# Expert layers: 32 x 32 turns on VectorE, stripes of 1024 hidden columns, longer runs in the weight loads

## Chip, cores and metric

One core of a Trainium2 chip runs the kernel. The metric is the device time of one execution in microseconds; the time before is the median of three runs.

## The reference

A decoder trunk of two layers on one sequence of 256 tokens with 1024 channels, all in float32. Each layer has a mixer part (a gated convolution, a state-space model and a sparse attention side by side, merged by gates) and then a feed-forward part. The first layer's is dense. The second layer's, which the change touches, sends each token to two of eight experts:

```python
def swiglu(h, w1, w3, w2):
    return (jax.nn.silu(h @ w1) * (h @ w3)) @ w2

def moe_ffn(h, router_w, w1, w3, w2):
    logits = (h @ router_w).astype(jnp.float32)
    vals, idx = lax.top_k(logits, TOP_K_EXPERTS)          # 2 of 8
    probs = jax.nn.softmax(vals, axis=-1)
    gate = jnp.sum(jax.nn.one_hot(idx, N_EXPERTS, dtype=jnp.float32) * probs[..., None], axis=-2)
    out = jnp.zeros_like(h)
    for e in range(N_EXPERTS):
        out = out + gate[..., e:e + 1] * swiglu(h, w1[e], w3[e], w2[e])
    return out
```

w1 and w3 of an expert are 1024 x 3584, w2 is 3584 x 1024: 44 MB an expert, 352 MB in all.

## The kernel before

The engines run programs of their own and meet through semaphores. SyncE loads all weights in 1 MB chunks into `raw`, a ring of six slots (`load_at`, L595): a slot is loaded again when `used` says that TensorE is done with it. A chunk of w1 or w3 holds 4 of the 8 blocks of 128 input channels by 512 hidden columns, so a partition gets four runs of 2 KB; a chunk of w2 holds 2 blocks of 128 hidden channels by 1024 outputs, two runs of 4 KB.

An expert takes at most 96 tokens (`SLOTS`). Its 3584 hidden columns are cut into 7 stripes of 512. TensorE's order for a stripe is: products with w1 (2 chunks, into bank 0 of PSUM), then the turn of the hidden values of the stripe before (`turn_hidden`, L1364: three 128 x 128 transposes through PSUM bank 4), products with w3 (2 chunks, bank 1), then the down products with w2 for the stripe before (2 chunks, banks 2 and 3, summed over all stripes). ScalarE applies silu to bank 0 (`silu`, L1886); VectorE multiplies by bank 1 (`times_up`, L2444) and copies the turned values from bank 4 to `hidT` (L2591). The first w1 and w3 stripe of the next expert come ahead of the last down products of an expert.

All products are made of `four_tiles`: the 96 tokens are three groups of 32 columns of the array. Each takes 384 of the 512 weight columns (L1333); the remaining 128 columns of all three groups go, one after the other, through the fourth 32 columns (L1336). The four parts of the array work side by side. Values thus lie in PSUM as three rows of tiles of 384 columns and a fourth with three times 128. A float32 matmul shows as two in the profile.

The tokens of the next expert: VectorE makes `pick`, TensorE finds their numbers in the second stripe (`find_tokens`), VectorE casts them (L2587), GpSimd gathers the rows from memory into `xg_tok` (L2909), and TensorE turns them behind w3 of the last stripe of an expert (`turn_gathered`, L1425: eight transposes into banks 6 and 7, copied to `xgT` by ScalarE and VectorE). An expert's output is copied to `y_sb` by ScalarE and stored to `y_rows` by GpSimd (L2835); for the last expert the stored rows of the others are gathered into `y_back` (L2916) and added by VectorE (`add_rows`), and its own output goes back through a scatter product. Rounds after the first (`rnd > 0`) run only if an expert has over 96 tokens. `y_taken`, `hid_done`, `sil_done` and `hidT_copied` guard the buffers.

## Time and profile before

| | us |
|---|---|
| median of three runs | 1647.84 (1646.87 to 1651.17) |
| the profiled execution, its time | 1651.2 |
| its span | 1649.4 |
| TensorE busy | 1614.8 |
| VectorE busy | 582.3 |
| ScalarE busy | 397.8 |
| GpSimd busy | 404.5 |
| first expert matmul | 714.41 |

Busy time of TensorE counts a matmul from start to modelled end, so that a stretch of 100% still has room. The DMA share counts the time of packets over 16 engines; packets in flight overlap, so it can stand above 1. In every slice from 700 us on the expert stage runs. How long a weight transfer takes to land, against how long the slot's turn lasts, tells how late the weights are.

### The profile page before, as it was taken

The page shows a single profiled execution, that of the slowest core. Times are in us where ns is not written, and L with a number is a line of the kernel's source. Part 1 is how long each engine was busy: PE and PEld are TensorE (multiplying, and loading weights), DVE is VectorE, ACT ScalarE, POOL GpSimd, SP SyncE. Part 2 cuts the span into 40 slices and gives each one's busy share as a digit, 9 for nine tenths or more (in the row PEclk, how much of TensorE's full clock was granted, in tenths as well). Part 3 has the DMA queues.
Part 4 walks back from the last instruction along what each step waited for, and adds up shares of the span by engine and source line. Part 5 has one row for each costly group of instructions (what it writes and reads, how often), then busy time and mean ns, then how long its engine had stood idle before and what let it go on. Part 6 is the DMA issues. An engine that isn't in the chain of part 4 may idle for free.

```text
span 1649.4 us, 46626 instructions
## 1 busy us (share of the span) xinstructions
PE 1614.8 (98%) x20940; PEld 1498.3 (91%) x20940; DVE 582.3 (35%) x784; ACT 397.8 (24%) x527; POOL 404.5 (25%) x541
## 2 busy tenths in 40 slices
PE   8999999999999999999999999999999999999998
PEld 5887888999978788899999999999999999999997
DVE  4799866466568977510000000000000000000002
ACT  4245455544454554510000000000000000000000
POOL 8856900999434523120000000000000000000100
PEclk9899999999999999999999999999999999999999
DMA  8453456556544455389999999999999999999996
GB/s 298 130 177 128 145 176 229 186 195 206 179 154 129 147 173 178 120 293 374 392 387 387 390 391 387 387 387 393 389 387 395 385 389 392 389 386 391 395 394 255
DMA packets 212094, 481.10 MB, mean 292 GB/s; under 512 B 7936, under 2 KB 32640, under 8 KB 211696
## 3 DMA queue, kind: packets, MB, share of 16 engines
q1 hardware_dynamic: 207456, 463.34, 77.4%
q0 software_dynamic: 4064, 14.95, 2.7%
q8 instruction: 122, 2.00, 0.5%
q10 hardware_dynamic: 432, 0.65, 0.1%
q14 instruction: 20, 0.16, 0.0%
HBM read 472.49 MB, written 6.42 MB: 290 GB/s over the span
## 4 chain that ended last, share of the span: by engine, by line
PE 67%; DVE 2%; DMA 1%; ACT 0%; issue 0%; DVEq 0%
PE ps L1336 33%; PE ps L1333 20%; PE ps L676 2%; PE ps L677 2%; PE ps L678 2%; PE ps L1364 2%; DMA raw<-moe_w 1%; PE ps L722 1%; PE ps L723 1%; PE ps L724 1%; DVE w_lo L306 1%; PE ps L912 0%; PE ps L1425 0%; PE ps L1300 0%; PE ps L1406 0%; DVE keybias L2169 0%
## 5 line engine op out<-in xcount | busy, mean ns | idle before, releaser
L1336 PE MATMUL ps<-raw,xgT 128*32 128x128 f32 x5424 | 611.6, 273 | 0.0
L1333 PE MATMUL ps<-raw,xgT 128*32 128x384 f32 x5424 | 604.2, 487 | 1.6 <-DMA raw<-moe_w 1.6
L1336 PEld LDWEIGHTS ps<-raw,xgT 128*32 128x32 f32 x5424 | 587.5, 110 | 0.0
L1336 PE MATMUL ps<-raw,hidT 128*32 128x128 f32 x2640 | 297.5, 273 | 0.0
L1333 PE MATMUL ps<-raw,hidT 128*32 128x384 f32 x2640 | 293.9, 486 | 0.0
L1336 PEld LDWEIGHTS ps<-raw,hidT 128*32 128x32 f32 x2640 | 287.5, 110 | 0.0
L306 DVE TENSOR_TENSOR w_lo<-raw,w_hi 128x2048 fp32r<-128x2048 f32 (+1 forms) x97 | 238.3, 2465 | 114.2 <-ACT w_hi L300 113.6
L2591 DVE COPY hidT<-ps 128x384 f32<-128x384 f32 x55 | 30.7, 558 | 564.1 <-PE ps L1364 564.1
L300 ACT ACTIVATE w_hi<-raw 128x2048 fp32r<-128x2048 f32 (+1 forms) x97 | 185.2, 1910 | 174.9 <-PE ps L678 83.4
L1333 PEld LDWEIGHTS ps<-raw,xgT 128*32 128x32 f32 x5424 | 215.9, 109 | 10.1 <-issue 9.8
L1886 ACT ACTIVATE sil<-ps 128x384 f32<-128x384 f32 (+1 forms) x67 | 33.9, 506 | 736.9 <-PE ps L1336 736.9
L2835 POOL DMA_DIRECT2D y_rows<-y_sb x7 | 3.8, 545 | 618.3 <-ACT y_sb L1976 618.3
L2444 DVE TENSOR_TENSOR hid<-sil,ps 128x384 f32<-128x384 f32 (+1 forms) x67 | 38.5, 574 | 279.6 <-PE ps L1336 277.3
L676 PE MATMUL ps<-w_hi,hT_hi 128*128 128x512 f32 (+1 forms) x264 | 105.7, 401 | 3.9 <-DVE uv L2155 3.2
L1333 PEld LDWEIGHTS ps<-raw,hidT 128*32 128x32 f32 x2640 | 106.8, 109 | 1.0 <-issue 0.2
L677 PE MATMUL ps<-w_lo,hT_hi 128*128 128x512 f32 (+1 forms) x264 | 103.8, 393 | 0.0
L678 PE MATMUL ps<-w_hi,hT_lo 128*128 128x512 f32 (+1 forms) x264 | 103.7, 393 | 0.0
L1224 PE MATMUL ps<-hT_hi,w_hi 128*128 128x256 f32 x336 | 95.2, 283 | 0.0
L1226 PE MATMUL ps<-hT_hi,w_lo 128*128 128x256 f32 x336 | 95.1, 283 | 0.0
L1228 PE MATMUL ps<-hT_lo,w_hi 128*128 128x256 f32 x336 | 95.1, 283 | 0.0
L722 PE MATMUL ps<-hT_hi,w_hi 128*128 128x256 f32 x224 | 64.9, 290 | 2.4 <-DVE w_lo L306 2.4
L676 PEld LDWEIGHTS ps<-w_hi,hT_hi 128*128 128x128 f32 x264 | 50.2, 190 | 16.1 <-DVE uv L2155 3.6
(417 smaller groups left out, 2253.1 us busy)
## 6 DMA issues: line engine op xcount, KB each, us to landing
raw<-moe_w SPq DMA_DIRECT2D x336, 1024.0 KB, 9.8
raw<-w_in SPq DMA_DIRECT2D x44, 1024.0 KB, 5.6
raw<-ffn_w SPq DMA_DIRECT2D x33, 1024.0 KB, 5.3
raw<-w_o SPq DMA_DIRECT2D x8, 1024.0 KB, 4.9
raw<-w_out_a SPq DMA_DIRECT2D x4, 1024.0 KB, 4.8
raw<-w_out_c SPq DMA_DIRECT2D x4, 1024.0 KB, 5.0
raw<-w_out_b SPq DMA_DIRECT2D x4, 1024.0 KB, 4.9
raw<-w_in SPq DMA_DIRECT2D x4, 904.0 KB, 4.8
```

The source lines that it names most:

```text
L300: act.activation(w_hi[:, n % SPLIT, 0:width], raw[:, n % RAW, 0:width], ACT.Copy)\
L306: dve.tensor_tensor(w_lo[:, n % SPLIT, 0:width], raw[:, n % RAW, 0:width], w_hi[:, n % SPLIT, 0:width].bitcast(F32), ALU.subtract)\
L676: pe.matmul(dst, x_hi, hi, start=first, stop=False, skip_group_check=True)
L677: pe.matmul(dst, x_hi, lo, start=False, stop=False, skip_group_check=True)
L678: return pe.matmul(dst, x_lo, hi, start=False, stop=last, skip_group_check=True)
L722: pe.matmul(dst, wh, x_hi[:, k0 + k, :], start=start, stop=False, skip_group_check=True)
L1224: pe.matmul(dst, hi[:, k, cols], hT_hi[:, k, :], start=k == 0 and c == 0, stop=False, skip_group_check=True)
L1226: pe.matmul(dst, lo[:, k, cols], hT_hi[:, k, :], start=False, stop=False, skip_group_check=True)
L1228: mm = pe.matmul(dst, hi[:, k, cols], hT_lo[:, k, :], start=False, stop=k == KD - 1, skip_group_check=True)
L1333: pe.matmul(ps[tile_rows(g), bank, 0:WIDE], x_of(g), w[:, 0:WIDE], start=first, stop=last, skip_group_check=True, tile_position=(0, TILE * g))
L1336: mm = pe.matmul(ps[SLOTS:P, bank, g * P:(g + 1) * P], x_of(g), w[:, WIDE:HALF], start=first and g == 0, stop=last, skip_group_check=True, ...
L2444: dve.tensor_tensor(hid[:, 0:width], sil[:, 0:width], ps[:, 1, 0:width], ALU.mult)\
```

## The change

- `HALVES = (2, 2, 2, 1)`: an expert has three stripes of 1024 hidden columns (pairs of halves of 512) and one of 512. TensorE's order for a pair is w1 (4 chunks, banks 0 and 1), w3 (4 chunks, banks 2 and 3), then the down products of the stripe before (4 chunks, or 2 for the half one; banks 4 and 5). SiLU and product take a pair in one instruction.
- The turns of hidden values and gathered rows leave TensorE. VectorE turns blocks of 32 by 32 from `hid_pair` to `hidT` (24 instructions of 32 x 128 for a pair) and from `xg_tok` to `xgT` (12 of 32 x 256).
- Chunks of w1 and w3 in pairs are 2 blocks of 128 input channels by 1024 columns (two runs of 4 KB a partition); the half stripe keeps 4 by 512. Chunks of w2 put four neighbouring hidden channels on one partition and take two of them (one run of 8 KB); the source of the turn is read with a stride of four to match.
- Down products are cut 388 + 3 x 124 in place of 384 + 3 x 128. Rank, token and pick banks move (2 to 4, 5 to 7), and the loops over stripes are written out.

```diff
-MOE_STRIPES = FF_EXPERT // HALF
+PAIR = 2 * HALF
+HALVES = (2, 2, 2, 1)
+MOE_STRIPES = len(HALVES)
+Y_WIDE = WIDE + 4
...
-            w2e = moe_w2[0].rearrange("e (k p) n -> p (e k) n", p=P)
+            w2e = moe_w2[0].rearrange("e (k p j) n -> p (e k) j n", p=P, j=4)
                 def up(m, turns, w, e, t):
-                    col = value(sp, t * HALF)
-                    for half in range(2):
-                        row = value(sp, KD * e + 4 * half)
-                        load_at(m + half, turns, w[:, bass.ds(row, 4), bass.ds(col, HALF)], used)
+                    ks = 4 // HALVES[t]
+                    for c in range(KD // ks):
+                        row = value(sp, KD * e + ks * c)
+                        load_at(m + c, turns, w[:, bass.ds(row, ks), t * PAIR:t * PAIR + HALVES[t] * HALF], used)
                 def down(m, turns, e, t):
-                    for half in range(2):
-                        row = value(sp, K2 * e + 4 * t + 2 * half)
-                        load_at(m + half, turns, w2e[:, bass.ds(row, 2), :], used)
+                    for c in range(2 * HALVES[t]):
+                        row = value(sp, K2 * e + 2 * t + c // 2)
+                        j = 2 * (c % 2)
+                        load_at(m + c, turns, w2e[:, bass.ds(row, 1), j:j + 2, :].rearrange("p o j n -> p (o j) n"),
+                                used)
...
-                def step(i, turns, middle=None, after=None):
-                    up(n0 + 4, 0, i + 1, turns)
-                    turn_hidden(i)
-                    if middle is not None:
-                        middle()
-                    up(n0 + 6, 1, i + 1, turns)
-                    if after is not None:
-                        after()
+                def step(n, i, turns, halves):
+                    up(n, 0, i + 1, turns, halves)
+                    up(n + 2 * halves, 1, i + 1, turns, halves)
                 def expert(e, last):
...
+                    step(n, i, turns, 2)
...
+                    down(n + 8, i + 1, turns, 2, first=True)
+                    n += 12
+                    step(n, i + 1, turns, 2)
+                    if not pick_turned:
+                        find_tokens(e + 1)
+                    down(n + 8, i + 2, turns, 2)
+                    n += 12
+                    step(n, i + 2, turns, 1)
...
+                    down(n + 4, i + 3, turns, 2)
+                    n += 8
                     if last:
-                        last_down(n0 + 4, i + t + 1, turns + t)
+                        last_down(n, i + 4, turns)
                     else:
+                        if rnd == 0:
+                            pe.wait_ge(S["xg_turned"], e + 1)
...
+                        step(n, i + 3, turns, 2)
+                        down(n + 8, i + 4, turns, 1)
...
+                def turn_gathered(e, w3_used):
+                    dve.wait_ge(S["xg_loaded"], value(dve, 16 * e))
+                    dve.wait_ge(used, value(dve, w3_used))
+                    for g in range(TILES):
+                        for q in range(4):
+                            src = xg_tok[tile_rows(g), :].rearrange("s (k q n) -> s k q n", k=KD, q=4)[:, :, q, :]
+                            ins = dve.transpose(xgT[tile_rows(q), :, tile_rows(g)], src)
+                    ins.then_inc(S["xg_turned"], 1)
+                def turn_hidden(at, halves, free, dst=hidT):
+                    dve.wait_ge(S["hid_done"], value(dve, at))
+                    if free is not None:
+                        dve.wait_ge(used, value(dve, free))
+                    turned = dst[:, 0:4 * halves * SLOTS].rearrange("p (c s) -> p c s", s=SLOTS)
+                    for h in range(halves):
+                        for g in range(TILES):
+                            for q in range(4):
+                                rows = tile_rows(g if q < TILES else TILES)
+                                col = h * WIDE + P * (q if q < TILES else g)
+                                src = hid_pair[rows, col:col + P].rearrange("s (n j) -> s j n", j=4)
+                                ins = dve.transpose(turned[tile_rows(q), 4 * h:4 * h + 4, tile_rows(g)], src)
+                    ins.then_inc(S["hidT_made"], 1)
...
+                def stripe(at, free, w3_at, before, halves):
+                    turn_hidden(at, before, free)
+                    times_pair(at + 1, w3_at, at - DENSE_STRIPES, halves)
...
+                    stripe(i + 1, n, n + 8, 2, 2)
...
+                    stripe(i + 2, n + 12, n + 20, 2, 2)
                     if rnd == 0 and not last:
...
                         tokens(e + 1)
...
                     if last and rnd == 0:
                         add_rows(0, 0)
+                    stripe(i + 3, n + 24, n + 28, 2, 1)
...
+                    if rnd == 0:
+                        turn_gathered(e + 1, n + 28)
...
+                    stripe(i + 4, n + 32, n + 40, 1, 2)
```

## Rows read from the trace of the kernel before

**Rows 1.** The page: busy us of each engine, then DMA share in 40 slices, in tenths.

```profile
PE 1614.8 (98%) x20940; PEld 1498.3 (91%) x20940; DVE 582.3 (35%) x784; ACT 397.8 (24%) x527; POOL 404.5 (25%) x541
DMA  8453456556544455389999999999999999999996
```

**Rows 2.** Waits in the expert stage: who for whom, total us, times, longest.

```profile
PE ps L1333 <- DMA raw<-moe_w: 1.6, 1, 1.6
...
SPq L595 <- PE ps L1336: 671.9, 325, 3.4
```

**Rows 3.** Chain that ended last: start us, us, what.

```profile
1049.25 0.81 PE ps L1425 x8
...
1126.28 0.48 PE ps L1364 x3
1142.62 0.48 PE ps L1364 x3
...
1164.81 0.81 PE ps L1425 x8
...
1542.54 15.44 DMA raw<-moe_w
...
1639.67 0.34 PE ps L1336 x3
```

**Rows 4.** DMA issues from 650, 720, 1200 and 1550 us: count, KB, us to landing.

```profile
raw<-moe_w SPq DMA_DIRECT2D x4, 1024.0 KB, 5.2
...
raw<-moe_w SPq DMA_DIRECT2D x11, 1024.0 KB, 6.6
...
raw<-moe_w SPq DMA_DIRECT2D x36, 1024.0 KB, 10.5
...
raw<-moe_w SPq DMA_DIRECT2D x18, 1024.0 KB, 12.5
```

**Rows 5.** Timeline of TensorE at a turn of hidden values: start us, us, what.

```profile
910.79 0.71 PE L1336 MATMUL ps<-raw,xgT 128*32 128x128 f32 x5
...
911.92 0.52 PE L1336 MATMUL ps<-raw,xgT 128*32 128x128 f32 x3
912.25 0.50 PE L1333 MATMUL ps<-raw,xgT 128*32 128x384 f32 x3
912.57 0.50 PE L1333 MATMUL ps<-raw,xgT 128*32 128x384 f32 x3
```

**Rows 6.** Stretches: busy us of each engine, granted clock, DMA share, GB/s.

```profile
235.00:238.00 3.00, 3.00 (x14) 2.41 (x13) 1.69 (x3) 0.00 (x0) 0.00 (x0) 1.00 1.06 355
1131.00:1138.00 7.00, 7.00 (x136) 7.00 (x131) 0.55 (x1) 0.00 (x0) 0.00 (x0) 1.00 1.05 387
1191.00:1194.00 3.00, 3.00 (x54) 2.63 (x46) 0.56 (x1) 0.49 (x1) 0.00 (x0) 1.00 1.03 416
1625.00:1628.00 3.00, 3.00 (x61) 3.00 (x57) 0.00 (x0) 0.00 (x0) 0.00 (x0) 1.00 1.03 411
717.00:950.00 233.00, 233.00 (x4139) 227.55 (x4134) 17.54 (x36) 10.27 (x21) 8.94 (x35) 1.00 1.03 382
```

**Rows 7.** First expert matmul, then DMA issues of gathered rows: count, us to landing.

```profile
714.41 0.52 PE L1333 MATMUL ps<-raw,xgT 128*32 128x384 f32 x3
...
xg_tok<-table_store,token_of POOLq DMA_INDIRECT x7, 7.8
...
y_back<-y_rows,row_of_choice POOLq DMA_INDIRECT x4, 9.3
```

**Rows 8.** Groups of VectorE by shape: count, busy us, mean ns, idle before.

```profile
L2591 DVE COPY hidT<-ps 128x384 f32<-128x384 f32 x55 | 30.7, 558 | 564.1 <-PE ps L1364 564.1
...
L2171 DVE TENSOR_TENSOR keybias<-keybias,causal 128x128 f32<-128x128 f32 x4 | 3.6, 910 | 0.1
...
L2587 DVE CAST token_of<-ps 96x1 int32<-96x1 f32 x7 | 1.0, 148 | 0.0
```

More of the change, by code:

```diff
@@ L197, in trunk @@
         ffn = ExitStack()
+        with ExitStack() as pairs:
+            sil_pair = sb("sil_pair", [P, 2 * WIDE], F32, pairs)
         sil = sb("sil", [P, HALF], F32, ffn)
@@ L201, in trunk @@
         upper = sb("upper", [P, P], F32, ffn)
+        with ExitStack() as pairs:
+            hid_pair = sb("hid_pair", [P, 2 * WIDE], F32, pairs)
         hid = sb("hid", [P, HALF], F32, ffn)
@@ new lines, in expert @@
+                def expert(e, last):
+                    turns = MOE_TURNS * e
+                    m = n + 8
+                    for t in range(1, MOE_STRIPES):
+                        up(m, turns, w1e, e, t)
+                        up(m + 2 * HALVES[t], turns, w3e, e, t)
+                        m += 4 * HALVES[t]
+                        down(m, turns, e, t - 1)
+                        m += 2 * HALVES[t - 1]
+                    if not last:
+                        up(m, turns, w1e, e + 1, 0)
+                        up(m + 4, turns, w3e, e + 1, 0)
+                        m += 8
+                    down(m, turns, e, LAST)
@@ L1305, in route @@
                 pe.wait_ge(S["upper_made"], 1)
-                pe.matmul(ps[:, 2, 24:25], upper[:, :], ones[:, 0:1], start=True, stop=True, skip_group_check=True)
+                pe.matmul(ps[:, 4, 24:25], upper[:, :], ones[:, 0:1], start=True, stop=True, skip_group_check=True)
                 turn_x(1, (1,))
@@ L1367, in down @@
-                def down(n, i, turns, first=False, middle=None):
-                    pe.wait_ge(S["hidT_copied"], i - DENSE_STRIPES)
-                    for chunk in range(2):
+                        for k in range(ks):
+                            kk = ks * c + k
+                            w = slot_view(raw, m, (ks, HALF * halves))[:, k, :]
+                            for half in range(halves):
+                                mm = four_tiles(2 * which + half, lambda g: xgT[:, kk, tile_rows(g)],
+                                                w[:, half * HALF:(half + 1) * HALF], kk == 0, kk == KD - 1)
@@ L1371, in down @@
+                        mm.then_inc(used, 1)
+                def down(n, i, turns, halves, first=False):
+                    pe.wait_ge(S["hidT_made"], i - DENSE_STRIPES)
+                    for chunk in range(2 * halves):
                         m = n + chunk
                         loaded(m, turns)
+                        turned = hidT[:, chunk // 2 * WIDE:(chunk // 2 + 1) * WIDE]
                         for k in range(2):
                             for half in range(2):
-                                mm = four_tiles(2 + half, hidden_tile(hidT, 2 * chunk + k),
+                                mm = four_tiles(4 + half, hidden_tile(turned, 2 * (chunk % 2) + k),
@@ L1470, in expert @@
                         pe.wait_ge(S["acc_done"], acc_before(rnd, e))
-                    down(n0 + 8, i + 1, turns, first=True)
-                    if last or rnd > 0:
+                    down(n + 8, i + 1, turns, 2, first=True)
+                    if pick_turned:
                         turn_pick(e)
-                    first = 2
-                    if rnd == 0 and not last:
-                        first = 3
-                        step(i + 1, turns + 1, middle=lambda: find_tokens(e + 1))
-                        down(n0 + 8, i + 2, turns + 1)
@@ L1479, in expert @@
-                    with pe.Fori(first, MOE_STRIPES - 1) as t:
-                        step(i + t - 1, turns + t - 1)
-                        down(n0 + 8, i + t, turns + t - 1)
-                    t = MOE_STRIPES - 1
-                    def next_tokens():
-                        if not last and rnd == 0:
-                            turn_gathered(e + 1)
-                        elif not last:
-                            pe.wait_ge(S["pickT_done"], scattered_before(rnd, e) + 1)
-                            gather(e + 1)
@@ L1493, in expert @@
-                    step(i + t - 1, turns + t - 1, after=next_tokens)
-                    down(n0 + 8, i + t, turns + t - 1, middle=(lambda: turn_hidden(i + t)) if last else None)
+                    n += 12
[5 more added lines that the diff above has]
+                    step(n, i + 2, turns, 1)
+                    if not last and rnd > 0:
+                        pe.wait_ge(S["pickT_done"], scattered_before(rnd, e) + 1)
+                        gather(e + 1)
@@ L2586, in tokens @@
                     dve.wait_ge(S["token_ps"], seen)
[L2587 to L2599 removed]
+                    dve.tensor_copy(token_of[0:SLOTS, :], ps[0:SLOTS, 7, TOKEN_AT:TOKEN_AT + 1]).then_inc(S["token_done"], 1)
@@ new lines, in times_pair @@
+                def times_pair(sil_seen, w3_used, turned, halves, lows=None):
+                    dve.wait_ge(S["sil_done"], value(dve, sil_seen))
+                    dve.wait_ge(used, value(dve, w3_used))
+                    if turned is not None:
+                        dve.wait_ge(S["hidT_made"], value(dve, turned))
+                    if lows is not None:
+                        dve.wait_ge(S["hidT_lo_done"], lows)
+                    dve.tensor_tensor(halves_of(hid_pair, halves), halves_of(sil_pair, halves), ps[:, 2:2 + halves, 0:WIDE],
+                                      ALU.mult).then_inc(S["hid_done"], 1)
```

224 lines of the change are left out of this document (94 added, 130 removed).

## The prediction

> **What bounds the kernel now.** I read the page first. TensorE is busy for 98% of the span; the DMA engines are full from 700 us on, through all the expert stage, and only there [rows 1]. Both cannot be the bound by accident, so the next views ask which of them ends last. The waits of TensorE name the weights once, for 1.6 us, in the whole expert stage, while the DMA queue of SyncE stands 671.9 us in 325 waits for TensorE to give a slot back [rows 2]. So TensorE sets the pace. The chain says the same: the turns of the gathered rows of two experts stand at 1049.25 and 1164.81, 115.56 us apart, and one stripe is 16.34 us (1126.28 to 1142.62) [rows 3]; the stripes that I compared are alike to 0.01 us. A pace that even is that of an engine that waits for nothing.
>
> But the weights are nearly late. From issue to landing a megabyte takes 6.6 us as the stage begins, 10.5 after 500 us, and 12.5 at its end [rows 4]. A slot is filled while five other chunks of 2.75 us are used, so 13.8 us is where lateness begins. At 1542.54 one transfer takes 15.44 us, and TensorE waits [rows 2, 3]. The change must therefore be priced on both: what TensorE saves counts only as far as the transfers follow.
>
> **TensorE's part.** One four-tile product is two passes; in each, three column groups take 384 columns side by side and the fourth takes three pieces of 128. The wide ones follow each other at 0.32 us (912.25, 912.57). The pieces: five last 0.71 us, of which the last one's own time is 0.27, so one starts every 0.11 us (the unrounded count is 0.109), three make 0.3275 us, and the fourth group is the slower one. A product is 0.655 us and the 24 of a stripe 15.73 us. The stripe is 16.34: the turn of the hidden values costs 0.6 us. The same is seen at the turn itself: the last piece starts at 911.23, its follower would start at 911.34 and starts at 911.92, behind the three transposes [rows 3, 5].
> - Removed: 7 such turns of an expert, 4.2 us.
> - Removed: the turn of the gathered rows. 115.56 less 7 x 16.34 is 1.18 us, in which is the finding of tokens too, which stays; the eight transposes alone stand in the chain with 0.81 [rows 3]. I take 0.9 us.
> - The down products are cut 388 + 3 x 124 in place of 384 + 3 x 128: wide 0.326 us, pieces 0.317 by scaling the columns, so 0.326 in place of 0.3275, and with 112 passes 0.17 us.
> - Together 5.3 us: an expert costs TensorE 110.3 us. Over eight experts and with the 1.6 us wait gone the last expert matmul, now at 1639.67 [rows 3], could end at 1595.7.
>
> **The transfers' part.** The rate by length of run, in stretches where only one length is in flight: 1 KB 355 GB/s, 2 KB 387, 4 KB 416 and 411 [rows 6] (at 235 us w1 and w3 of the dense part are loaded, at 1131 those of an expert, at 1191 and 1625 its w2; TensorE's granted clock is 1.00, 2.4 GHz, in each). Per run and engine (16 engines) this is 46.2, 84.5 and 158.5 ns, a line with some 9 to 10 ns of fixed cost and 36 to 37 ns for a KB. 8 KB isn't in the trace as a weight load. Bounds: no gain at all (413 GB/s) and the last step carried on (303 ns, 433 GB/s). I take the whole line, 308 ns or 425 GB/s.
> - Now: 28 up chunks at 2.706 us (1.0486 MB at 387.5 GB/s) and 14 down chunks at 2.536 us (at 413.5): 111.3 us per expert.
> - What it really needs: the chunk that arrives at 1557.98 is the 300th after the first that had to wait for a slot (TensorE begins at 714.41 with six chunks in place, so that one is issued at 717.0; with 5.2 us from issue to landing, as before the stage [rows 4], it is there at 722.2). In between also came four gathers of 128 rows of 4 KB, 2.1 MB or 5.1 us at 411 GB/s. (1557.98 - 722.2 - 5.1) / 300 is 2.769 us, 116.3 us per expert [rows 3, 6, 7]. So 5.0 us an expert are for other things: stored and gathered rows (0.79 MB, 2 us), TensorE's instructions, the first stretch at 382 GB/s.
> - After: 24 up chunks in runs of 4 KB (60.9 us), 4 up chunks of the single last half stripe still in 2 KB (10.8), 14 down chunks in 8 KB at 2.467 (34.5), 5.0 for the rest, and 0.2, an estimate, because TensorE's loop over stripes is written out and more instructions are fetched: 111.4 us, 2.652 us a chunk.
> - So the transfers are 1.1 us an expert slower than TensorE and become the bound once the head start is used up (13.8 - 5.2, less what the gathers at the end take). Last chunk there: 722.2 + 329 x 2.652 + 5.1 - 2.0 (the last expert stores and gathers nothing) = 1597.8; TensorE then has 3.9 us of the last down products: 1601.7. Against 1639.7 that is 38 us less.
>
> The Trainium skill ("DMA: Bandwidth & Descriptors", Bandwidth) has a rule that speaks against this half of the change: HBM gives one core about 358 GB/s, and for loads from HBM that side binds, not the engines. The trace disagrees: 382 to 416 GB/s for hundreds of us [rows 6]. By that rule the 352 MB of expert weights would need an estimated 984 us, longer than the whole stage takes now, so it drops out of the sum and of the chances.
>
> **VectorE's part.** Its new work is beside TensorE, in windows that follow from the new order. A turn of a pair of stripes is 24 instructions of 32 x 128, a single one's is 12, and the gathered rows are 12 of 32 x 256. No row shows such an instruction. From below: the 96 x 1 cast, 148 ns. From above: 128 columns at the worst rate per column, 910 ns. The nearest is the 384-column copy, 558 ns: (558 - 148) / 383 is 1.07 ns a column, so 284 ns for 128 and 421 for 256 [rows 8]; I take these. Then 24 are 6.8 us and the gathered rows 5.1 us.
> - Widest cover: the first two turns of an expert and the last have the following w1 and w3, 21 us.
> - Narrowest: the third pair's turn starts when the second down products are done, and the third down products wait for it; between lie the four up chunks of the half stripe, 10.5 us. 24 instructions fit up to 437 ns.
> - The gathered rows are turned between the last w3 of an expert and the next expert's w1, which is four down chunks, 10.4 us, after one product of some 1 us: they fit up to 0.78 us each. The gather itself lands after some 8 us [rows 7] and has 21.
> - Behind these on VectorE stand the products of pairs, which TensorE needs a whole w1 later, and ScalarE's one activation of 768 columns in place of two of 384. I cost all of it at nothing. In the last expert add_rows waits for the gathered outputs ahead of the third turn; they are there some 22 us after the sixth expert ends, its turn 50 us later.
> - The move of the rank, token and output banks changes addresses alone: nothing, bounded by one matmul either way.
>
> **The sum.** Profiled execution 1651.2 us (span 1649.4): 1651.2 - 38 = 1613. This execution is 3.4 us over the median of the runs; the median after is 1647.84 - 38 = 1610, and I say 1611, as single stalls between the two equal paces can only add.
>
> **The rivals.**
> - *TensorE stays the bound*, because the rest of 5.0 us shrinks along with the count of packets. For it: the fixed cost is per run and the runs are halved. Against it: landing times rise already now. Gives 1647.84 - 44 = 1604.
> - *8 KB gives less than hoped*: at 4 KB's rate 112 chunks cost 0.07 us more each, 7.8 us, so 1618. Or worse, because partitions of the down weights now lie 16 KB apart and only half of each is read by a transfer; at 2 KB's rate it would be 112 x 0.24 = 27 us, 1637, the far bound. For it: no row shows such a load. Against: every longer run in the trace was faster. (The Trainium skill, "DMA: Bandwidth & Descriptors", Latency and other measured facts, tells of lost bandwidth at row pitches of 512 KiB and above, 207 for 214 GB/s at 512 KiB; 16 KB is far below. No run here shows it; by that ratio 3.4% of 34.5 us would be 1.2 us an expert.)
> - *The transfers do not gain at all*, that is, the runs' length isn't what holds them and TensorE's saving turns into waits for weights: 116.3 us an expert goes on, last chunk at 722.2 + 329 x 2.769 + 3.1 = 1636.3, TensorE at 1640: no change, 1646. Against it: the rate steps with each length.
> - *VectorE's turns come too late* (the other side). Place: third down products of each expert, which wait for hidT_made. Each instruction over 437 ns costs 24 times its excess, 8 times. The gain of 38 us is gone at 4.75 us an expert, 635 ns each. At the upper bound of 910 ns, 11.4 us an expert there and 0.8 us more for the other turn (21.8 against 21), some 98 us: 1708. For it: the sources are read with a stride of four words, and one VectorE form of 128 columns takes 910 ns [rows 8]. Against: most rows are near 1.07 ns a column.
>
> **Chances.** Forecast 0.57 (its own range 1605 to 1617), TensorE bound 0.13, 8 KB poor 0.17, no gain in transfers 0.05, VectorE late 0.08 (of which 0.02 stays short of the break-even). Range 1602 to 1632: outside it lie the last two cases and the tail of the third. What can be told from no change here is 0.3%, 5 us. Faster by more: the first three cases, 0.02 of the last and 0.01 of the fourth, 0.90; within: 0.03 of the fourth; slower: 0.07.
>
> **What would show it.** Expert period 111 to 112 us in the chain, without L1364 and L1425; first experts at 110.3 with landings that climb from 6 to 13 us, and after that small waits of TensorE for weights, 5 to 8 us in all; 410 GB/s or more in down stretches and above 400 over the stage; VectorE's turns at 250 to 300 ns, and no wait of TensorE for hidT or xgT. It is wrong if waits of TensorE name VectorE, if the GB/s stay at 390, or if a four-tile product isn't 0.655 us once the turns no longer part the stripes.

## The result, and the profile after

| | before | after |
|---|---|---|
| median | 1647.9 (1646.87 to 1651.17, 4 runs) | 1622.33 (1617.45 to 1622.77, 4 runs) |
| ratio to before, 95% interval | | 0.9835 [0.9811, 0.9858] |
| profiled execution, its span | 1651.2, 1649.4 | 1617.45, 1615.6 |
| first expert matmul | 714.41 | 707.93 |
| last expert matmul ends about | 1640.0 | 1606.5 |
| the stage between them | 925.6 | 898.6 |

The change saves 25.6 us of the median. The two profiled executions are 33.8 us apart, which flatters it: after's began the experts 6.5 us earlier, although nothing ahead of them is changed. Up to 720 us the granted clock stood at 1.2 GHz for some 28 us before and 18 after (from 700 to 717 us its mean is 0.90 and 1.00), which is worth 5 of the 6.5 us. The expert stage alone gained 27.0 us where 38 were forecast.

The head of the page of after, to set beside [rows 1]:

```profile
span 1615.6 us, 46115 instructions
PE 1573.0 (97%) x20716; PEld 1463.8 (91%) x20716; DVE 854.8 (53%) x1453; ACT 390.4 (24%) x496; POOL 409.0 (25%) x541
...
GB/s 304 179 135 131 144 175 237 183 182 216 181 182 106 170 151 163 158 235 395 389 410 413 394 413 397 400 407 387 406 412 389 403 411 392 405 409 393 408 404 258
```

TensorE is still busy for 97% and the memory rate is above 390 GB/s in most slices, so the page again doesn't say which of the two ends last. Between 900 and 1500 us TensorE, which was busy for the whole 600 us before, now is for 593.5. The starts of the gathered rows' turn on VectorE (start us, length us, what) give the expert period, as the two L1425 pieces did in [rows 3]:

```profile
803.15 5.37 DVE L2598 STREAM_TRANSPOSE xgT<-xg_tok 32x256 f32<-32x256 f32 x12
...
913.09 5.37 DVE L2598 STREAM_TRANSPOSE xgT<-xg_tok 32x256 f32<-32x256 f32 x12
...
1025.42 5.37 DVE L2598 STREAM_TRANSPOSE xgT<-xg_tok 32x256 f32<-32x256 f32 x12
```

The first step is 109.94 us, the second 112.33; the next four are 112.51, 112.50, 112.21 and 112.45. The first expert goes at TensorE's own pace, the others at another. Which one, the waits of TensorE and of its weight loads say (total us, times, longest), the answer to [rows 2]:

```profile
PEld ps L1356 <- DMA raw<-moe_w: 11.5, 18, 2.3
...
PE ps L1356 <- DMA raw<-moe_w: 10.0, 21, 2.0
...
PEld ps L1356 <- DVE hidT L2613: 1.6, 3, 0.6
```

TensorE now waits for weights some twenty times, each time briefly; VectorE's late hidden values cost 1.6 us in the whole stage. The landing times of the weights issued from 750 to 800, 900 to 1000 and 1400 to 1500 us, where [rows 4] had 6.6 climbing to 12.5:

```profile
raw<-moe_w SPq DMA_DIRECT2D x19, 1024.0 KB, 7.7
...
raw<-moe_w SPq DMA_DIRECT2D x39, 1024.0 KB, 12.5
...
raw<-moe_w SPq DMA_DIRECT2D x37, 1024.0 KB, 12.6
```

They climb fast and then stand still at 12.5 to 12.8 us, just short of the 13.8 at which lateness begins (weights issued from 1000 to 1300 us take 12.8); a backlog that no longer grows is one that the consumer waits for. The rates by stretch (columns as in [rows 6]): the long mean, a gather of rows beside the stream, the 8 KB runs, and two stretches of 4 KB runs:

```profile
900.00:1500.00 600.00, 593.48 (x10799) 581.20 (x10794) 240.73 (x564) 25.60 (x42) 7.39 (x10) 1.00 1.02 402
1120.50:1123.50 3.00, 3.00 (x63) 2.83 (x55) 0.00 (x0) 0.00 (x0) 0.00 (x0) 1.00 1.03 256
1134.00:1137.00 3.00, 3.00 (x62) 2.96 (x53) 2.01 (x5) 0.00 (x0) 0.00 (x0) 1.00 1.03 423
1145.00:1157.00 12.00, 11.68 (x217) 11.36 (x218) 4.97 (x12) 0.00 (x0) 0.00 (x0) 1.00 1.03 410
1202.00:1212.00 10.00, 9.87 (x181) 9.30 (x176) 5.50 (x14) 0.00 (x0) 0.00 (x0) 1.00 1.02 406
```

The 423 GB/s are three good microseconds. Two other stretches in which only runs of 8 KB are in flight:

```profile
1336.00:1339.00 3.00, 3.00 (x60) 2.95 (x56) 0.00 (x0) 0.00 (x0) 0.00 (x0) 1.00 0.97 381
1359.00:1362.00 3.00, 3.00 (x63) 2.97 (x59) 2.47 (x6) 0.00 (x0) 0.00 (x0) 1.00 0.98 410
```

Looked at in steps of 1 us, the 30 stretches of 3 us with (nearly) only 8 KB runs between 900 and 1500 us lie between 371 and 426 GB/s, with a mean of 411; the 104 with only 4 KB runs have a mean of 408.

The costliest VectorE group of the change, the turn of hidden values, at 417 ns each:

```profile
L2613 DVE STREAM_TRANSPOSE hidT<-hid_pair 32x128 f32<-32x128 f32 x660 | 275.4, 417 | 225.4 <-PE ps L1359 216.7
```

And the chain of waits (start us, us, what) names such a turn in the first two experts and after them weight transfers, most of 12.8 to 14.3 us:

```profile
902.21 0.41 DVE hidT L2613
...
1337.24 13.83 DMA raw<-moe_w
```

### The profile page after: what moved, and what is told of

It reads as the page before. It is cut to its first block, busy times and chain, and to the rows that moved or that the text cites. A ratio compares the mean times of both kernels' runs of the same rounds, so it can differ in the third digit from the quotient of the medians.

```text
span 1615.6 us, 46115 instructions
## 1 busy us (share of the span) xinstructions
PE 1573.0 (97%) x20716; PEld 1463.8 (91%) x20716; DVE 854.8 (53%) x1453; ACT 390.4 (24%) x496; POOL 409.0 (25%) x541
## 4 chain that ended last, share of the span: by engine, by line
PE 50%; DMA 15%; DVE 4%; issue 0%; ACT 0%; SPq 0%; DVEq 0%
PE ps L1359 23%; PE ps L1356 15%; DMA raw<-moe_w 15%; PE ps L698 2%; PE ps L699 2%; PE ps L700 2%; DVE hidT L2613 1%; PE ps L744 1%; PE ps L745 1%; PE ps L746 1%; DVE w_lo L325 1%; PE ps L934 1%; PE ps L1423 0%; DVE keybias L2173 0%; PE ps L1315 0%
## 5 line engine op out<-in xcount | busy, mean ns | idle before, releaser
L1356 PE MATMUL ps<-raw,xgT 128*32 128x384 f32 x5424 | 594.1, 487 | 6.8 <-DMA raw<-moe_w 6.5
L1359 PE MATMUL ps<-raw,xgT 128*32 128x128 f32 x5424 | 600.1, 273 | 0.0
L1359 PEld LDWEIGHTS ps<-raw,xgT 128*32 128x32 f32 x5424 | 587.7, 110 | 0.0
L2613 DVE STREAM_TRANSPOSE hidT<-hid_pair 32x128 f32<-32x128 f32 x660 | 275.4, 417 | 225.4 <-PE ps L1359 216.7
L1356 PE MATMUL ps<-raw,hidT 128*32 128x388 f32 x2640 | 295.2, 490 | 4.2 <-DMA raw<-moe_w 3.5
L1359 PE MATMUL ps<-raw,hidT 128*32 128x124 f32 x2640 | 287.5, 269 | 0.0
L1359 PEld LDWEIGHTS ps<-raw,hidT 128*32 128x32 f32 x2640 | 277.3, 110 | 0.0
L1356 PEld LDWEIGHTS ps<-raw,xgT 128*32 128x32 f32 x5424 | 227.3, 109 | 14.7 <-issue 8.9
L1970 ACT ACTIVATE sil_pair<-ps 128x768 f32<-128x768 f32 (+1 forms) x32 | 23.4, 732 | 709.0 <-PE ps L1359 709.0
L2624 DVE TENSOR_TENSOR hid_pair<-sil_pair,ps 128x768 f32<-128x768 f32 (+1 forms) x32 | 27.3, 854 | 311.2 <-PE ps L1359 310.9
L1356 PEld LDWEIGHTS ps<-raw,hidT 128*32 128x32 f32 x2640 | 109.6, 109 | 10.7 <-DMA raw<-moe_w 7.6
L2939 POOL DMA_INDIRECT xg_tok<-table_store,token_of x7 | 6.7, 960 | 371.1 <-DVE token_of L2589 371.1
## 6 DMA issues: line engine op xcount, KB each, us to landing
raw<-moe_w SPq DMA_DIRECT2D x336, 1024.0 KB, 12.5
```

Source lines behind the costliest of these rows:

```text
L1356: pe.matmul(ps[tile_rows(g), bank, 0:wide], x_of(g), w[:, 0:wide], start=first, stop=last, skip_group_check=True, tile_position=(0, TILE * g))
L1359: mm = pe.matmul(ps[SLOTS:P, bank, g * rest:(g + 1) * rest], x_of(g), w[:, wide:HALF], start=first and g == 0, stop=last, skip_group_check ...
L2613: ins = dve.transpose(turned[tile_rows(q), 4 * h:4 * h + 4, tile_rows(g)], src)
```

## The experiments

The theory after the result was that transfers set the pace at 112.5 us an expert, with TensorE some 2.5 us faster behind them. Rivals were VectorE's turns (the chain names them), TensorE itself being slower than forecast, and the gather's dip. Each kernel below is the changed one with one edit, or with two where w2 is half loaded besides; periods are the distances of the gathered rows' turns as above. Ratios are to the kernel before on the same chip, whose median was 1646.0 us beside e0 to e3, 1646.4 beside e4 to e7 and 1647.0 beside e8 to e10.

**e0, the changed kernel once more.** No edit.

> The changed kernel once more, as the base for the others on the same chip: 1622 by all theories, period 112.4 from the third expert on.

1619.92 us (1615.03 to 1621.26), ratio 0.9839 [0.9822, 0.9856]; periods 110.01, 112.41, 112.36, 112.76, 112.75, 112.75. The 110 and the 112.5 are no accident of one execution (the last five have a mean of 112.61 here and 112.40 in the execution above).

**e1, the turns on VectorE and the new stripes, but the old run lengths** (2 KB for w1 and w3, 4 KB for w2). The turn follows the old order of rows; that part of the edit is not shown.

```diff
-                    ks = 4 // HALVES[t]
-                    for c in range(KD // ks):
-                        row = value(sp, KD * e + ks * c)
-                        load_at(m + c, turns, w[:, bass.ds(row, ks), t * PAIR:t * PAIR + HALVES[t] * HALF], used)
+                    for c in range(2 * HALVES[t]):
+                        row = value(sp, KD * e + 4 * (c % 2))
+                        col = t * PAIR + c // 2 * HALF
+                        load_at(m + c, turns, w[:, bass.ds(row, 4), col:col + HALF], used)
...
-            w2e = moe_w2[0].rearrange("e (k p j) n -> p (e k) j n", p=P, j=4)
+            w2e = moe_w2[0].rearrange("e (k p) n -> p (e k) n", p=P)
```

> The order of stripes and the turns on VectorE stay, the weights are loaded again as in the kernel before: up chunks in runs of 2 KB, down chunks in runs of 4 KB; the turn of hidden values follows the old order of rows, 32 instructions of 32 x 96 without a stride. Theory A (the transfers are the bound of the changed kernel; their price is set by the run length): expert period back to 116 us, landings of 13 us, over 40 us of waits for weights, about 1645, no faster than before by more than 5 us. Theory B (VectorE's turns, which fill 10.3 of 10.5 us, hold TensorE and are what is missing in the gain): the same as the changed kernel or faster, 1615 to 1622, since the turn has no stride here.

1650.26 us (1644.29 to 1654.23), ratio 1.0025 [1.0012, 1.0037]: TensorE's lighter load alone brings nothing, and even costs some 4 us. Its period, and the waits that took the saving:

```profile
1036.15 5.36 DVE L2593 STREAM_TRANSPOSE xgT<-xg_tok 32x256 f32<-32x256 f32 x12
...
1152.51 5.37 DVE L2593 STREAM_TRANSPOSE xgT<-xg_tok 32x256 f32<-32x256 f32 x12
```

```profile
PEld ps L1354 <- DMA raw<-moe_w: 38.3, 38, 2.9
PE ps L1354 <- DMA raw<-moe_w: 28.2, 42, 2.6
```

116.36 us between these two and 116.28 in the mean of the last five, where the kernel before needed 115.56 [rows 3]. The waits for weights are longer and more than in the change (38.3 against 11.5 us), and transfers take 13.7 us to land: what TensorE no longer does it spends waiting. The forecast had put the transfers' own need with the old runs at 116.3 us; this is that number measured. The kernel before hid it, for it began with a head start that was used up only near its end: landings climb from 6.6 to 12.5 us [rows 4], and the one wait stands at 1542.54 [rows 3]. The turn here reads its source without a stride, 96 columns at a time, and takes

```profile
L2607 DVE STREAM_TRANSPOSE hidT<-hid_pair 32x96 f32<-32x96 f32 x660 | 177.5, 269 | 240.0 <-PE ps L1357 231.5
```

against 417 ns for 128 columns with a stride of four: also no bound.

**e2, all of the change but the 8 KB runs** (w2 in 4 KB, hidden values in plain order, their turn without a stride as in e1).

```diff
-            w2e = moe_w2[0].rearrange("e (k p j) n -> p (e k) j n", p=P, j=4)
+            w2e = moe_w2[0].rearrange("e (k p) n -> p (e k) n", p=P)
...
-                        row = value(sp, K2 * e + 2 * t + c // 2)
+                        row = value(sp, K2 * e + 8 * t + 2 * c)
```

> Only the down weights are loaded as before, in runs of 4 KB with the old order of rows (and the turn without a stride); up chunks stay at 4 KB. Theory A: 112 down chunks at 4 KB's rate cost 0.07 us more each, period 113.4, 8 us slower than the changed kernel: 1630. Theory C (8 KB brings nothing, since down stretches of the changed kernel show 400 to 418 GB/s and dips): within 2 us of the changed kernel, 1622.

1625.40 us (1623.38 to 1626.36), ratio 0.9878 [0.9863, 0.9893].

```profile
1140.68 5.37 DVE L2596 STREAM_TRANSPOSE xgT<-xg_tok 32x256 f32<-32x256 f32 x12
...
1254.22 5.37 DVE L2596 STREAM_TRANSPOSE xgT<-xg_tok 32x256 f32<-32x256 f32 x12
```

Period 113.54 between these two, 113.27 in the mean of the last five: Theory A's 113.4, though its 1630 us was 5 too many. So from e1 to e2 the longer runs of w1 and w3 bring 24.9 us of median (192 chunks, 0.130 us each), and from e2 to e0 the 8 KB runs of w2 bring 5.5 (112 chunks, 0.049 us each). By the periods it is 3.0 us an expert (0.125 a chunk) and 0.7 to 0.9 (0.05 to 0.06). e0's strided turns cost it 1.5 us of waits for hidden values that e2 does not have, so the 8 KB runs alone may be worth a little more.

The whole gain came with the longer runs. But it needs both halves of the change: before, TensorE waited for weights once, for 1.6 us [rows 2], so quicker transfers alone had hardly more to give back. That is argued from the waits; the kernel with longer runs and the turns left on TensorE was not run.

**e3, half of each w2 chunk loaded**, so that transfers cannot bind. TensorE works on what lies there.

```diff
-                        load_at(m + c, turns, w2e[:, bass.ds(row, 1), j:j + 2, :].rearrange("p o j n -> p (o j) n"),
+                        load_at(m + c, turns, w2e[:, bass.ds(row, 1), j:j + 1, :].rearrange("p o j n -> p (o j) n"),
```

> The changed kernel, but each down chunk loads only the first of its two rows (half of the bytes; the output is then not the reference's). This takes 15% of the traffic away and lets the transfers run ahead. Theory A: TensorE sets the pace, period 109.9 to 110.3 for all experts, landings of 5 to 7 us, no waits for weights, 15 to 20 us faster than the changed kernel: 1603 to 1607. Theory B: period stays at 111 us or more and TensorE's waits name hidT.

1602.40 us (1601.69 to 1604.51), ratio 0.9740 [0.9727, 0.9753].

```profile
1025.89 5.37 DVE L2598 STREAM_TRANSPOSE xgT<-xg_tok 32x256 f32<-32x256 f32 x12
...
1135.83 5.37 DVE L2598 STREAM_TRANSPOSE xgT<-xg_tok 32x256 f32<-32x256 f32 x12
```

```profile
PEld ps L1356 <- DVE hidT L2613: 3.9, 8, 0.5
```

The period is 109.94 us, the same in every expert, and no wait for weights is left in it. This is TensorE's pace when weights are never late, 0.4 us under the forecast's 110.3. It refutes the rival that TensorE itself was slower than worked out. One wait is in it: VectorE's third turn ends late, and the weight loads stand 0.5 us for it, eight times. The wide matmuls on either side start 0.64 us apart (1134.66 and 1135.30) in place of 0.33, so some 0.3 us an expert is lost.

**e4, the dip of the gather.** The 96 rows are fetched by a plain transfer of the first rows of the table in place of the indirect one.

```diff
-                pool.indirect_dma_start(xg_tok[:, :], None, h_rows,
-                                        bass.IndirectOffsetOnAxis(token_of[0:SLOTS, 0:1], 0))\
+                pool.dma_start(xg_tok[:, :], h_rows[0:SLOTS, :])\
```

> The changed kernel, but GpSimd loads the 96 rows of the next expert by a plain transfer of the first 96 rows of h in place of the indirect gather (same bytes, other tokens: the output is then not the reference's). In the changed kernel the rate falls from 400 to about 240 GB/s for 3 us at each gather. Theory D (the indirect gather itself slows the weight stream; it is a part of the 6.2 us of rest per expert): the dip goes, period 111.3 in place of 112.5, 6 to 8 us faster than the changed kernel: 1613. Rival E (any row traffic from GpSimd costs so): the dip stays, 1620.

1618.51 us (1617.01 to 1622.66), ratio 0.9837 [0.9817, 0.9858], no different from e0: Rival E. The same three microseconds:

```profile
1120.50:1123.50 3.00, 2.56 (x47) 2.10 (x38) 0.00 (x0) 0.00 (x0) 0.00 (x0) 1.00 1.02 272
```

272 GB/s against 256 in the changed kernel, and the same period (112.54 in the mean of the last five). These are totals, the rows among them: the weight stream itself moved 0.42 MB of the changed kernel's 3 us, 140 GB/s, and 0.55 MB of these. That the rate falls beside the gather is so; the indirect addressing is at most a small part of it. What the dip comes from stays open: the rows cross the same engines as the stream in either form.

**e5, eight more turns of 32 x 128 ahead of the third turn of an expert,** into free columns of `hidT`'s memory.

```diff
+                    for x in range(spare):
+                        at_x = 2 * WIDE + P * (x // 4)
+                        dve.transpose(hidT_all[tile_rows(x % 4), at_x:at_x + P].rearrange("p (c s) -> p c s", c=4),
+                                      hid_pair[0:TILE, 0:P].rearrange("s (n j) -> s j n", j=4))
...
-                    turn_hidden(at, before, free)
+                    turn_hidden(at, before, free, spare=8 if (before, halves) == (2, 1) else 0)
```

> The changed kernel with 8 more 32 x 128 turns (into unused space) ahead of the third turn of each expert, the one with 10.5 us of cover: it then takes 13.6 us. Theory A (the transfers are the bound; TensorE has 2.5 us an expert to spare against them): TensorE's pace becomes 109.9 + 3.1 = 113.0, half a us over the transfers' 112.5; 3 us each in the first two experts, 0.5 to 1 in the others: 7 to 10 us slower than the changed kernel, 1628. Theory B (VectorE already holds TensorE): the full 3.3 us eight times, 26 us: 1646.

1645.92 us (1640.3 to 1651.36), ratio 0.9995 [0.9979, 1.0011]. The whole gain is gone: my number was 1628. The wait itself is what eight turns of 417 ns give, 3.3 us on top of 0.4:

```profile
PEld ps L1357 <- DVE hidT L2618: 29.8, 8, 3.8
```

What I had left out shows in the windows before, in and after one such wait (here, as in each row, the number before the DMA share is the granted clock):

```profile
1130.00:1140.00 10.00, 10.00 (x194) 10.00 (x189) 6.62 (x16) 0.49 (x1) 0.00 (x0) 1.00 1.05 386
1140.00:1147.00 7.00, 3.58 (x68) 3.21 (x63) 6.75 (x18) 0.00 (x0) 0.00 (x0) 0.91 1.01 415
1147.00:1160.00 13.00, 13.00 (x194) 12.40 (x191) 5.47 (x13) 0.00 (x0) 0.00 (x0) 0.79 0.86 314
```

The granted clock has two levels, 2.4 and 1.2 GHz, so a mean of 0.79 over the 13 us behind the wait is 5.5 us of them at the lower one (13 x 0.21 x 2). The 0.91 of the 7 us before is 1.3 us more, nearly all within the wait. The period is

```profile
1147.25 5.37 DVE L2599 STREAM_TRANSPOSE xgT<-xg_tok 32x256 f32<-32x256 f32 x12
...
1263.19 5.37 DVE L2599 STREAM_TRANSPOSE xgT<-xg_tok 32x256 f32<-32x256 f32 x12
```

115.94 us, 6.0 over e3. The longer wait is 3.2 of it (29.8 / 8 less e3's 3.9 / 8), and 5.5 us at half speed cost 2.7. Not every expert pays both: the first period is 113.17 us, with the clock at 1.00 behind the wait, the second 114.88, the other four 115.93 to 116.04.

**e6, the same eight turns with w2 half loaded.**

```diff
+                    turn_hidden(at, before, free, spare=8 if (before, halves) == (2, 1) else 0)
...
-                        load_at(m + c, turns, w2e[:, bass.ds(row, 1), j:j + 2, :].rearrange("p o j n -> p (o j) n"),
+                        load_at(m + c, turns, w2e[:, bass.ds(row, 1), j:j + 1, :].rearrange("p o j n -> p (o j) n"),
```

> The same 8 more turns in the kernel whose down chunks load half of their bytes (output not the reference's), where the transfers are far ahead. By the measured 417 ns and a cover of 10.5 us the wait of TensorE for hidT is 3.1 us an expert: period 113.1, 25 us over the 1602 of the half-loading kernel: 1627. If waits overlap with other slack, less than 15 us.

1645.32 us (1638.0 to 1647.13), ratio 0.9988 [0.9975, 1.0]: the same as e5 although its transfers are far ahead, so in both kernels it is TensorE with its waits, not the transfers, that sets the time. Against e3 this is 43 us more, of which eight waits of 3.2 us are 26. It missed its number (1627) by the rest. The periods are 113.20, 114.90, 116.42, 113.18, 114.90 and 116.04. Behind the third wait and behind the fourth:

```profile
1036.00:1049.00 13.00, 13.00 (x193) 12.41 (x197) 5.66 (x13) 0.00 (x0) 0.00 (x0) 0.78 0.59 212
```

```profile
1152.00:1165.00 13.00, 12.60 (x235) 12.60 (x239) 7.84 (x19) 0.00 (x0) 0.00 (x0) 1.00 0.79 298
```

The same wait in the same place, and once the clock falls and once it doesn't. Of the 16 such waits in e5 and e6, 13 were followed by 3.4 to 6.8 us at 1.2 GHz and three by none.

**e9, three more turns in place of eight, w2 half loaded,** to part the wait from the clock.

```diff
-                    turn_hidden(at, before, free)
+                    turn_hidden(at, before, free, spare=3 if (before, halves) == (2, 1) else 0)
```

> The half-loading kernel (output not the reference's) with 3 more turns ahead of the third turn of each expert in place of 8. With 8, TensorE waited 3.4 to 3.8 us once an expert, the granted clock then fell to 1.2 GHz for 6.8 us in most experts, and the period was 116.0 in place of 113.1. Theory F (a single wait of that length is what drops the clock): 3 more turns give a wait of some 1.5 us without a drop, period 111.2, 1612 to 1615. Rival (any wait here costs double): period 112.5, 1622.

1610.36 us (1608.53 to 1612.31), ratio 0.9773 [0.9758, 0.9788].

```profile
1027.15 5.37 DVE L2599 STREAM_TRANSPOSE xgT<-xg_tok 32x256 f32<-32x256 f32 x12
...
1138.32 5.37 DVE L2599 STREAM_TRANSPOSE xgT<-xg_tok 32x256 f32<-32x256 f32 x12
```

```profile
PEld ps L1357 <- DVE hidT L2618: 13.7, 8, 1.7
```

Waits of 1.7 us, period 111.17: 1.23 us over e3, three turns of 417 ns (1.25) and nothing more. The granted clock stays at 2.4 GHz through the stage. So eight waits of 1.7 us were each paid once, while those of 3.4 to 3.8 us in e5 and e6 cost between once and nearly twice their length, as the clock fell behind them or not (43 us for 26 from e3 to e6).

**e10, w2 half loaded and the down products cut 384 + 3 x 128 as before.**

```diff
-Y_WIDE = WIDE + 4
+Y_WIDE = WIDE
```

> The half-loading kernel (output not the reference's) with the down products cut 384 + 3 x 128 again. TensorE alone sets its pace there, so the cut shows: by the sum 112 passes of 1.5 to 1.9 ns, 0.17 to 0.2 us an expert, period 110.1 in place of 109.93, 1.5 us in all. Rival (the fourth column group doesn't set the pace once turns no longer part the stripes): no difference.

1607.07 us (1602.04 to 1607.45), ratio 0.9751 [0.9737, 0.9765].

```profile
1022.10 5.37 DVE L2598 STREAM_TRANSPOSE xgT<-xg_tok 32x256 f32<-32x256 f32 x12
...
1132.86 5.37 DVE L2598 STREAM_TRANSPOSE xgT<-xg_tok 32x256 f32<-32x256 f32 x12
```

Period 110.76 (110.77 in the mean of six) against 109.94 in e3: the four columns are worth 0.83 us an expert, where I had 0.17.

**e7, six more chunks of head start.** The memory of `w_hi` and `w_lo`, idle in this stage, takes chunks 7 to 12 once.

```diff
+                elif at < 2 * RAW:
+                    sp.wait_ge(used, MOE0 - 2 + (at - RAW) // 2)
+                    dst = spare[at - RAW][:, 0:k * w].rearrange("p (k n) -> p k n", k=k)
+                    sp.dma_start(dst, src).then_inc(S[SPARE_FULL[at - RAW]], 16)
```

> The changed kernel with six more megabytes prefetched: chunks 7 to 12 of the expert stage go to the memory of w_hi and w_lo, which the stage doesn't use, and the first six no longer wait for TensorE's last use but for the end of the split. Theory A (the transfers bound the stage, so whatever they do before it counts in full): the stream starts some 10 us earlier in full and the end moves by that: 1608 to 1612, with landings below 13 us for longer. Rival: no gain, because the end is set by TensorE and VectorE: 1620.

1620.57 us (1617.95 to 1622.94), ratio 0.9843 [0.9823, 0.9862]: nothing gained, and the periods are 110.08, 113.09, 112.38, 112.44, much as in e0. Landing time of what is issued from 800 to 900 us:

```profile
raw<-moe_w SPq DMA_DIRECT2D x38, 1024.0 KB, 10.6
```

The fault lies in the kernel, not in the theory: behind the six extra chunks the ring still has six slots, so the stream stands still while the extra ones are used up, and the start gained is given back. In the stretch behind the extra chunks it moves almost nothing:

```profile
730.00:740.00 10.00, 10.00 (x190) 10.00 (x188) 8.32 (x19) 0.00 (x0) 0.00 (x0) 1.00 0.07 28
```

28 GB/s, where the changed kernel has 385. It took a ring that stays deeper:

**e8, a ring of twelve slots through the whole stage.** SyncE's loop over the experts is also written out.

```diff
+        def expert_slot(at):
+            turn, place = at // (2 * RAW), at % (2 * RAW)
+            if place >= RAW:
+                return spare[place - RAW], S[SPARE_FULL[place - RAW]], 16 * (turn + 2)
+            m0 = MOE0 + place
+            return raw[:, m0 % RAW, :], raw_full[m0 % RAW], 16 * (m0 // RAW + 1 + turn)
...
+                else:
+                    sp.wait_ge(used, MOE0 + at - 2 * RAW + 1)
```

> The changed kernel with a ring of twelve slots of 1 MB through the whole expert stage (six of raw, six in the memory of w_hi and w_lo), not only six more chunks once. In the kernel with the deeper start alone the ring behind it had six slots, so the stream stood still until the second six had been used, and landings were again 10.6 us at 800 to 900 us. Theory A (transfers are the bound by 2.5 us an expert, TensorE's own pace being 109.9): the stream starts 10 to 13 us earlier and never has to wait, TensorE's waits for weights fall from 20 us to under 5, stage end set by TensorE: 1604 to 1609. Rival: the lag comes from what each transfer costs TensorE, not from the sum of the transfers: 1620.

1604.67 us (1603.87 to 1607.6), ratio 0.9743 [0.9727, 0.9759]: 43 us faster than before and 15 faster than e0.

```profile
1024.00 5.37 DVE L2642 STREAM_TRANSPOSE xgT<-xg_tok 32x256 f32<-32x256 f32 x12
...
1133.93 5.37 DVE L2642 STREAM_TRANSPOSE xgT<-xg_tok 32x256 f32<-32x256 f32 x12
```

```profile
PEld ps L1400 <- DVE hidT L2657: 4.0, 8, 0.5
PEld ps L1400 <- DMA spare_all<-moe_w: 3.8, 4, 2.2
```

The period is 109.93 and stays there; weights are waited for only at the very end. The stream isn't faster for it (401 GB/s from 900 to 1500 us, 402 in the changed kernel). It is ahead by more: the window from 690 to 717 us, just before the experts begin, in the changed kernel and then in this one:

```profile
690.00:717.00 27.00, 26.64 (x288) 24.38 (x291) 6.97 (x38) 10.90 (x20) 10.91 (x30) 1.00 0.52 183
```

```profile
690.00:717.00 27.00, 27.00 (x270) 24.97 (x272) 7.19 (x38) 10.89 (x20) 9.89 (x26) 0.94 0.79 287
```

183 against 287 GB/s, idle memory time put to use. Then the backlog grows (issued from 800, 1000 and 1400 us):

```profile
raw<-moe_w SPq DMA_DIRECT2D x18, 1024.0 KB, 11.0
...
raw<-moe_w SPq DMA_DIRECT2D x20, 1024.0 KB, 16.7
...
raw<-moe_w SPq DMA_DIRECT2D x18, 1024.0 KB, 20.2
```

The head start is used up bit by bit, and with twelve slots it lasts nearly to the end. By the periods of e0 each expert should use up some 2.5 us of it; the landings grow by 1 to 3 us an expert, so I can't say that the deeper queue has gained no rate at all. It is the best version of the study.

## Why the prediction was right or wrong

- **Which engine binds.** Right: transfers take over after the first expert. Waits for weights, landings that climb and stop, e3 and e8 show it; the range held the time and the sign was right. The waits came to 10.0 us, where 5 to 8 had been named.
- **TensorE's pace, 110.3 us.** Measured 109.94 (e3), and it is luck that it came so near: terms were off against each other. Cut 388 + 3 x 124: 0.83 for 0.17 us (e3 against e10), with what VectorE's third turn takes back already off. I had scaled each wide matmul and taken the larger of two nearly equal times, pass by pass. From this row on it is only argued: wide ones and pieces may run apart over a long stretch, and then what counts is the total of each part of the array, not the larger in every pass. The fourth part has 112 x 12 columns less to do, an estimated 1.14 us at 0.109 us for 128; less the 0.3 us that TensorE then stands for VectorE's third turn (e3) this is 0.84. The turns removed: 115.56 - 110.77 (e10, old cut) is 4.8 us in place of the forecast's 5.1. And the wait for VectorE had been put at nothing.
- **Transfers' pace, 111.4 us: the step that failed,** with 112.4 to 112.6 measured. The mechanism was right (the gain by the length of a run), its size too large. The 24 up chunks were priced at 2.536 us by 413.5 GB/s, the mean of two stretches of 3 us with down chunks in the kernel before. They are two of the fastest of their kind: looked at in steps of 1 us, the 18 stretches of 3 us with (nearly) only 4 KB runs between 800 and 1630 us have a mean of 405, and two of them are

```profile
826.00:829.00 3.00, 3.00 (x63) 3.00 (x56) 0.00 (x0) 0.00 (x0) 0.00 (x0) 1.00 1.03 404
1624.00:1627.00 3.00, 3.00 (x60) 3.00 (x56) 0.12 (x1) 0.00 (x0) 0.00 (x0) 1.00 1.01 401
```

  In the changed kernel stretches of 4 KB runs stand at 410 and 406, with 408 as the mean of all; at 408 a chunk is 2.570 us, and 24 of them are 0.8 us more. The 8 KB runs were priced at 0.069 us under 4 KB by a line through the shorter ones and brought 0.049 (e2 to e0), 0.3 us more over 14 chunks. Together 1.1 us an expert, and times 7.8 experts 8.6 of the missing 11 us. The "5.0 for the rest" held: e1 was forecast with it at 116.3 us and measured 116.28. The 0.2 us for fetched instructions was a guess with no row behind it; the pages show 2.80 MB of instructions after and 2.16 before, at 402 GB/s 0.2 us an expert. The stretch of 8 KB at 423 GB/s looks like my 425, but it is one of the fastest again: the mean of all is 411.
- **The last expert.** The fetch of stored rows (`y_back`) falls into it. The products of pairs on VectorE (L2624) at 1451.89 and 1569.10 are 117.2 us apart, 4.7 more than the other periods, where 5.1 - 2.0 = 3.1 had been forecast: 1.6 us of the miss. In e3, where transfers don't bind, the same two are 110.4 us apart, so the stretch lies in the transfers; what in it costs more than forecast wasn't tried. About 1 us is left over without a cause.
- **VectorE's turns, 284 ns.** Measured 417 for 32 x 128 with a source stride of four, 269 for 32 x 96 without. The plain rate per column was wrong for the strided form by half, and the cover of 437 ns held by 20 ns: 24 x 417 is 10.0 us (10.3 with the gaps) of 10.5. Even so the third turn came late: TensorE's weight loads stood 1.6 us for it in the changed kernel, where transfers bind, and 0.5 us an expert where they don't (e3, e8). The forecast had no such wait, and had named one as a sign of being wrong. The gathered turn: 435 to 450 ns for 421.
- **The price of a late turn** was wrong in the rival. It was a sum of waits: 24 x 8 x the excess over 437 ns, which for eight more turns (an average of 556 ns over the 24) is 23 us. From e3 to e6, where only the turns differ, it is 43 us: 26 of waits, and the rest goes with the clock that fell behind most of them. The break-even of 635 ns also rested on a gain of 38 us, of which there were 26. And the far bound counted one of the two turns under wide cover: with both it is 105 us, not 98.
- **The other rivals.** "TensorE stays the bound" isn't what the change does, but its 1604 is what e3 and e8 measure. "The transfers don't gain at all" is what e1 does, with 1650. "8 KB gives less than hoped" is true in size: 0.049 of 0.069 us.
- **The sum.** 38 us forecast, 27 in the profiled stage, 25.6 in the median: 11 us over the forecast of 1611, inside its range, outside its own narrow one.

## What to carry to other kernels

When two resources run within 1% of each other, lightening one moves nothing: price both and look for the one that is late next, here by an expert period that changes after the first expert. Between a fast consumer and a slightly slower stream, a deeper ring can buy what a better rate doesn't, as long as the stage is short and memory stands idle ahead of it: look for dead buffers. A rate that many chunks are priced by should come from all stretches of its kind, not from the two that look clean. And where work slides off the bottleneck onto a neighbour, work out the cover in that order's narrowest place, for once it is late, the wait is not all that it costs.

## What the runs showed of the hardware that was not expected

- Load rate by length of the run, in stretches of 3 us or more with one length in flight: 2 KB 387 GB/s [rows 6], 4 KB about 408, 8 KB 371 to 426 with a mean of 411. In the kernel a megabyte in 4 KB runs took 0.130 us less than in 2 KB, and in 8 KB 0.049 less than in 4 KB. A megabyte is 32 runs of 2 KB on each of the 16 engines, 16 of 4 KB or 8 of 8 KB; by the 16 and the 8 runs saved, a run has a fixed cost of an estimated 8 and 6 ns, where the prediction's line had 9 to 10. The Trainium skill ("HBM Reference", Specifications (TRN2)) says that a core which streams alone measures about 425 GB/s, bounded by its DMA engines, and gives the 358 that I weighed in the prediction as the share when both cores of a pair stream. The fastest stretches of 8 KB, 423 and 426 GB/s, agree with the first, and the mean over 600 us is 402; no run here has a second core.
- Waits of TensorE up to 2.3 us (after) and 1.7 (e9) left its granted clock at 2.4 GHz. Of 16 waits of 3.4 to 3.8 us (e5, e6) 13 were followed by 3.4 to 6.8 us at 1.2 GHz and three by none. What decides was not tried; the length of the wait alone does not.
- A gather of 96 rows of 4 KB takes the total rate from about 400 to 256 GB/s for 3 us, rows included, and a plain transfer of as many rows to 272.
- VectorE's 32 x 32 turns: 269 ns for 96 columns without a stride, 417 for 128 columns with a stride of four, 435 to 450 for 256 columns in unstrided blocks. The Trainium skill ("VectorE: DVE Perf Modes", The three transpose paths) gives 311 ns for VectorE's blocks of a 128 x 128 bf16 tile; no run here has that form, and the float32 ones differ by half among themselves. The stride seems to cost more than the columns; one form with one stride is too little to say how it grows, or that it isn't the form.
